# Decoder step on one core: VectorE subtracts the normalized stream, two bias tables behind one block each, six weight slots behind the skewed table's store

## The chip, the cores and the metric

The kernel runs on one core of a Trainium2 chip. The metric is the device time of one execution in microseconds (us), and lower is better. The kernel before took 2029.69 us (median of 3 runs, 2027.88 to 2030.03).

## What is computed

A two-layer decoder step over 576 tokens (one prompt of 512, eight sequences of 8 new tokens). Layer 0 mixes with a Mamba-2 state space scan, layer 1 with sparse attention; each is followed by a layer norm, an MLP with squared ReLU and another layer norm. All is float32. The part that matters here, cut from the reference:

```python
def layer_norm(x, g, b):
    xf = x.astype(jnp.float32)
    mu = jnp.mean(xf, axis=-1, keepdims=True)
    var = jnp.mean(jnp.square(xf - mu), axis=-1, keepdims=True)
    return ((xf - mu) * lax.rsqrt(var + LN_EPS)).astype(x.dtype) * g + b

def sq_relu_mlp(x, w1, w2):
    return jnp.square(jax.nn.relu(x @ w1)) @ w2

def run_group(...):
    ...
    for i in range(DEPTH):
        ...
        h = layer_norm(DN_ALPHA * h + mix, ln_g[i, 0], ln_b[i, 0])
        h = layer_norm(DN_ALPHA * h + sq_relu_mlp(h, mlp_w1[i], mlp_w2[i]), ln_g[i, 1], ln_b[i, 1])
```

The attention of layer 1 adds a bias that depends on the distance between two positions: `rel_bias` (32 buckets, 16 heads), looked up by `rel_bucket(dist)`.

## The kernel before

**Layout.** The residual stream `xT` lies in SBUF as 8 chunks of 128 features by 576 tokens. Every large projection goes over weight *slots* of 128x1024 floats (512 KB), streamed from HBM in one fixed order. One slot is the weights of 128 outputs over 1024 inputs.

**Precision.** A product is made of three: each operand is a rounded upper part plus the difference to it (the lower part), and `dense_block` (L1339) adds upper x upper, upper x lower and lower x upper, so one slot costs 48 matmuls of 288 columns. The upper part of a slot is made by ScalarE (`split_hi`, L975), the lower part, raw minus upper, by GpSimd (`split_lo`, L724). Slots lie in a ring of two: SyncE loads slot s+2 when slot s has been split (`stream`, L627), ScalarE rounds slot s when TensorE has used slot s-2, GpSimd subtracts, TensorE multiplies.

**One MLP** (`mlp`, `raw_projection` and `projection` on TensorE) goes in two halves of the 4096 hidden features: first product of half 0 (16 slots, one per block), second product of half 0 (8 blocks of 2 slots), first product of half 1, second product of half 1. The first product of half 0 starts on the stream before it is normalized; the layer norm's factors are put in behind the product. Meanwhile VectorE (`normalize`, L2172 and L2174) subtracts the mean and multiplies by the scale, chunk by chunk.

**The stretch in question** is the start of the second product of half 0, in layer 0 (slots called S+0 to S+15 here, S = `S_M2[k][0]`) and again in layer 1. Slots S+0 and S+1 are split inside the loop before. Then ScalarE (`mlp_his`, L1189 to L1209) makes for each of the 8 chunks two passes of `normalized`: one writes the rounded upper part of the normalized stream into `XM[k]` (L1184; `XM[0]` is `xs`, `XM[1]` is `xs_b`), one writes the float32 stream in place (L1185). It does five chunks, rounds slot S+2, does three chunks, rounds slot S+3. GpSimd (`mlp_los` with `x_los`, L837) makes the lower part of five chunks, then of slot S+2, then of three chunks, then of slot S+3. These lower parts are needed only by the first product of half 1, 14 slots later.

VectorE adds each finished block onto the stream (`residual`, L1969), in place; block 0 may be added when its chunk's lower part is made.

**Bias tables**, layer 0 only. Behind the second block, TensorE makes the strip table (three products into `bS` and `bXM`, L1672), VectorE copies it out (L2233 to L2235), TensorE then makes the compressed table into `bS` (L1677), VectorE copies it (L2237). SyncE stores the strip table (65 KB, L641), loads two slots, writes it 128 times over as a skewed table of 3 MB from HBM to HBM (L645), loads two slots, waits for that store, loads 2 MB of it as strips (L649), then stores and reloads the compressed table in small pieces (L656, L663) and copies 16 rows (L671), with two slots between each four of them. All this is in SyncE's one queue with the weights. The waits are semaphores written out by hand; nothing is scheduled by a planner.

Of the kernel before, what the change touches and what calls it, by code (L numbers as in the profile page):

```python
# [24 lines left out]
F32 = mybir.dt.float32  # L25
F32R = mybir.dt.float32r
I32 = mybir.dt.int32
ALU = mybir.AluOpType
# [5 lines left out]
KC = D // P  # L34
# [35 lines left out]
NSLOT = 2  # L70
# [15 lines left out]
def build(nc, a):  # L86

    with ExitStack() as ctx:
# [54 lines left out]
        xT = carve(KC, T)  # L143
# [473 lines left out]
        @block.sync  # L617
        def _(sp):
            for j in range(NSLOT):
                sp.dma_start(ring[:, j, :], a["w"][j, :, :]).then_inc(w_ready[j], 16)  # L620

            def stream(first, last):
                with sp.Fori(first // NSLOT, last // NSLOT) as i:
                    for j in range(NSLOT):

                        sp.wait_ge(w_split, i * NSLOT + (j + 1 - NSLOT))
                        sp.dma_start(ring[:, j, :], a["w"][i * NSLOT + j, :, :]).then_inc(w_ready[j], 16)  # L627

            for dst, name in PARAM_TILES[1:]:
                sp.dma_start(dst, a[name]).then_inc(s_par, 16)  # L630
            stream(NSLOT, S_OUT[0] + 2 * NSLOT)

            sp.wait_ge(xbc_ready, NXB)
            sp.wait_ge(y_gated, (MG - 1) * NT)
            sp.dma_start(xT, a["x"]).then_inc(x_back, 16)
            s_bias = S_M2[0][0] + 4 * NSLOT
            stream(S_OUT[0] + 2 * NSLOT, s_bias)


            sp.wait_ge(bt_ready, 1)  # L640
            sp.dma_start(a["bscr"], bt).then_inc(bt_stored, 16)  # L641
            stream(s_bias, s_bias + NSLOT)
            y0 = Y0 - 2 * P + 1
            sp.wait_ge(bt_stored, 16)
            sp.dma_start(a["bskew"], bass.AP(a["bscr"].tensor, y0, [[0, P], [XN, NH], [1, RW]])  # L645
                         ).then_inc(skew_stored, 16)
            stream(s_bias + NSLOT, s_bias + 2 * NSLOT)
            sp.wait_ge(skew_stored, 16)
            sp.dma_start(Rs, bass.AP(a["bskew"].tensor, P - 1, [[NH * RW - 1, P], [RW, NH], [1, RB]])  # L649
                         ).then_inc(strips_loaded, 16)  # L650


            s_next = s_bias + 2 * NSLOT
            sp.wait_ge(bt_ready, 2)
            for qa in range(8):
                sp.dma_start(bass.AP(a["bscr"].tensor, (7 - qa) * CS * NH, [[NH, CS], [8 * CS * NH, 8], [1, NH]]),  # L656
                             btT[qa * CS:(qa + 1) * CS]).then_inc(bt_stored, 16)
                if qa % 4 == 3:
                    stream(s_next, s_next + NSLOT)
                    s_next += NSLOT  # L660
            sp.wait_ge(bt_stored, 16 * 9)
            for pa in range(8):
                sp.dma_start(cbt[pa * CS:(pa + 1) * CS], bass.AP(a["bscr"].tensor, (63 - 55 - pa) * CS * NH,  # L663
                                                                 [[NH, CS], [CS * NH, NSIG], [1, NH]])
                             ).then_inc(cbt_ready, 16)
                if pa % 4 == 3:
                    stream(s_next, s_next + NSLOT)
                    s_next += NSLOT
            sp.wait_ge(strips_loaded, 16)
            for h in range(NH):  # L670
                sp.dma_start(nr[h * NS:(h + 1) * NS, :], Rs[0:NS, h, 0:P + 2 * NS]).then_inc(rows_loaded, 16)  # L671
                if h % 4 == 3:
                    stream(s_next, s_next + NSLOT)
                    s_next += NSLOT
            stream(s_next, S_O + 2 * NSLOT)

            sp.wait_ge(s_ptab, 16)

            for b in range(NB):
                buffer_free(sp, b, True)  # L680
                for pg in range(NPG):
                    page = sp.value_load(ptab[0:1, b * NPG + pg:b * NPG + pg + 1], min_val=0, max_val=NPHYS - 1)
                    sp.dma_start(skv[b % KVB][:, pg, :], a["sel"][page, :, :]).then_inc(kv_loaded[b % KVB], 16)
            stream(S_O + 2 * NSLOT, N_SLOTS)

            for m in range(0, KC, 2):
                sp.wait_ge(x_ready, 3 * KC + m + 2)
                sp.dma_start(a["o_y"][:, m:m + 2, :], xT[:, m:m + 2, :]).then_inc(x_out, 16)
            sp.wait_ge(x_out, 16 * KC // 2)
# [3 lines left out]
        def _(pool):  # L693
# [135 lines left out]
            pool.wait_ge(sd_stored, 16 * MG)  # L829
            pool.wait_ge(outs, 48)  # L830

            def x_los(k, first, last):


                for m in range(first, last):
                    pool.wait_ge(x_ready, 2 * k * KC + m + 1)
                    pool.tensor_tensor(XM[k][:, 1, m, :], xT[:, m, :], XM[k][:, 0, m, :].bitcast(F32), ALU.subtract  # L837
                                       ).then_inc(x_split, 1)

            def mlp_los(k, half, end):  # L840

                with pool.Fori(0, H1 // NSLOT) as i:
                    for j in range(NSLOT):
                        split_lo(S_M1[k][half] + 2 + j, i)

                        pool.wait_ge(hid_hi, i * NSLOT + ((2 * k + half) * H1 + j + 1))
                        m = i * NSLOT + j
                        pool.tensor_tensor(HID[k][1][:, m, :], sq[:, j, :], HID[k][0][:, m, :].bitcast(F32),
                                           ALU.subtract).then_inc(hid_ready, 1)
                if half:  # L850
                    finish_los(2 * k + 1)
                else:
                    s0 = S_M2[k][half] + 2
                    x_los(k, 0, 5)
                    split_lo(s0)
                    x_los(k, 5, KC)
                    split_lo(s0 + 1)
                    split_los(s0 + 2, end)


            pool.wait_ge(blk_evac, B_OUT[1] + KC)
# [100 lines left out]
        def _(act):  # L962
# [224 lines left out]
            def mlp_his(k, half, end):  # L1187
# [10 lines left out]
                if half:  # L1198
                    finish_his(2 * k + 1)
                else:  # L1200
                    s0 = S_M2[k][0] + 2
                    act.wait_ge(w_used, S_M2[k][0])
                    for m in range(5):
                        normalized(2 * k, m, XM[k])
                    split_hi(s0)
                    for m in range(5, KC):
                        normalized(2 * k, m, XM[k])
                    split_hi(s0 + 1)
                    split_his(s0 + 2, end)  # L1209

            root_of_variance(0)
# [128 lines left out]
        def _(pe):  # L1340
# [27 lines left out]
            def projection(b0, s0, blocks, nsl, hi, lo, ready=None, raw=0, between=None):  # L1368

                for j in range(2):  # L1370
                    dense_block(b0 + j, s0 + j * nsl, nsl, hi, lo, ready=ready if j == 0 else None, raw=raw)
                if between:
                    between()
                with pe.Fori(1, blocks // 2) as i:
                    for j in range(2):
                        dense_block(b0 + j, s0 + j * nsl, nsl, hi, lo, i, 2 * nsl, raw=raw)
# [285 lines left out]
                    mm = pe.matmul(flat_s[:, cols], ones[0:TQ, :], CEN[k][0:TQ, cols], start=True, stop=True)  # L1662
                mm.then_inc(ln_wide, 1)

            def bias_tables():

                pe.wait_ge(s_tab, 16 * N_ATT)
                pe.wait_ge(ln_scaled, 2 * KC)
# [1 line left out]
                for i, (bank, lo) in enumerate(((bS[:, 0, :], 0), (bS[:, 1, :], 512), (bX[:, :], 1024))):  # L1670
                    n = min(512, XN - lo)
                    pe.matmul(bank[0:NH, 0:n], relb[:, :], eb[:, lo:lo + n], start=True, stop=True  # L1672
                              ).then_inc(bt_done, 1)

                pe.wait_ge(bt_ready, 1)
                for i in range(8):
# [4 lines left out]
            def mlp(k):  # L1681

                raw_projection(2 * k, B_M1[k][0], S_M1[k][0], H1)
                projection(B_M2[k][0], S_M2[k][0], KC, 2, *HID[k], (hid_ready, 2 * k * H1),
                           between=bias_tables if k == 0 else None)
                pe.wait_ge(x_split, NORM_LO[k] + KC)
                projection(B_M1[k][1], S_M1[k][1], H1, 1, XM[k][:, 0], XM[k][:, 1])
                last_projection(2 * k + 1, *HID[k], (hid_ready, (2 * k + 1) * H1))
# [233 lines left out]
        def _(dve):  # L1922
# [179 lines left out]

            def residuals(k, between=None):

                b0, s0 = B_M2[k][0], S_M2[k][0]
                for j in range(2):
                    dve.wait_ge(x_split, NORM_LO[k] + j + 1)
                    residual(b0 + j, j, ALPHA, s0 + (j + 1) * 2)
                if between:
                    between()  # L2110
                with dve.Fori(1, KC // 2) as i:
                    for j in range(2):
                        dve.wait_ge(x_split, at_step(NORM_LO[k] + j + 1, i, 2))
# [113 lines left out]
                    if half == 0:  # L2227
                        normalize(2 * k, 0, i)

            def bias_tables():  # L2230

                dve.wait_ge(bt_done, 3)
                dve.tensor_copy(bt[:, 0:512], bS[0:NH, 0, :])  # L2233
                dve.tensor_copy(bt[:, 512:1024], bS[0:NH, 1, :])
                dve.tensor_copy(bt[:, 1024:XN], bX[0:NH, 0:XN - 1024]).then_inc(bt_ready, 1)  # L2235
                dve.wait_ge(cbt_done, 1)
                dve.tensor_copy(btT.rearrange("p s h -> p (s h)"), bS[:, 0, 0:8 * NH]).then_inc(bt_ready, 1)  # L2237

# [1 line left out]
            layer_norm(0)  # L2240
            mlp_hidden(0, 0)

            residuals(0, bias_tables)
            mlp_hidden(0, 1)
            last_residuals(1)
            layer_norm(1)
# [410 lines left out]
```

## Time and profile before

| | before |
|---|---|
| median of 3 runs | 2029.69 us (2027.88 to 2030.03) |
| the profiled execution | 2017.36 us, span 2015.7 us |
| TensorE busy | 1897.1 us, 94% of the span |
| VectorE, ScalarE, GpSimd busy | 983.7, 738.9, 889.7 us |
| mean granted TensorE clock | 0.97 |
| DMA | 185.14 MB, 92 GB/s mean |

The span is from the first to the last instruction of the profiled execution, and that execution's own time is 1.7 us more. [...] "Released by" is the instruction whose semaphore ended a wait. Matmul ends are modelled.

### The profile page before, as it was taken

The numbers are of one execution on the slowest core, as the hardware profiler recorded it, in microseconds if no ns is written. First come the engines' busy times: TensorE is split into PE (matmuls) and PEld (weight loads), VectorE is DVE, ScalarE is ACT, GpSimd is POOL, SyncE is SP. The second block draws the span as 40 slices with busy tenths as digits, with TensorE's granted clock in tenths as the row PEclk, the third lists the DMA queues.
The fourth block names the chain that finished last, engine by engine and source line by source line (L and its number), as shares of the span: only waits on it lengthen the run. The fifth ranks groups of instructions, "written<-read, shape, count | busy, mean of one in ns | idle before, by whom it ended". The sixth has DMA issues, their size and how long they took to land. (4 is left out here: it accounts for less than half of the span.)

```text
span 2015.7 us, 36867 instructions
## 1 busy us (share of the span) xinstructions
PE 1897.1 (94%) x14678; PEld 1738.9 (86%) x14678; DVE 983.7 (49%) x1762; ACT 738.9 (37%) x1346; POOL 889.7 (44%) x644
## 2 busy tenths in 40 slices
PE   8999989979899998999999999799879999999996
PEld 7987878758799988999999989555459999999996
DVE  6375866756576500121456731577457652012134
ACT  5474636532233431222221141466444334122222
POOL 3544343342475552565443323444305456346552
PEclk9999989989999999999999989799999999999998
DMA  5213113141322217522222434600431222222221
GB/s 188 66 64 112 68 42 126 53 152 53 111 86 83 75 64 181 131 75 83 84 74 83 145 104 106 230 1 1 143 132 63 73 83 74 76 82 83 84 79 62
DMA packets 61223, 185.14 MB, mean 92 GB/s; under 512 B 15662, under 2 KB 20430, under 8 KB 59568
## 3 DMA queue, kind: packets, MB, share of 16 engines
q1 hardware_dynamic: 50432, 130.92, 20.3%
q0 software_dynamic: 9952, 50.08, 7.2%
q10 hardware_dynamic: 720, 2.49, 0.3%
q8 instruction: 83, 1.36, 0.3%
q14 instruction: 36, 0.29, 0.0%
HBM read 167.05 MB, written 27.35 MB: 96 GB/s over the span
## 5 line engine op out<-in xcount | busy, mean ns | idle before, releaser
L1361 PE MATMUL dense<-xs,split 128*128 128x288 f32 x5056 | 722.7, 300 | 2.3 <-DVE xs L2461 2.3
L1361 PEld LDWEIGHTS dense<-xs,split 128*128 128x128 f32 x5056 | 693.7, 191 | 30.0 <-issue 29.9
L724 POOL TENSOR_TENSOR split<-ring,split 128x1024 fp32r<-128x1024 f32 x174 | 434.7, 2499 | 568.0 <-ACT split L975 567.9
L975 ACT ACTIVATE split<-ring 128x1024 fp32r<-128x1024 f32 x212 | 224.2, 1058 | 700.8 <-PE dense L1361 668.2
L1969 DVE SCALAR_TENSOR_TENSOR tile<-tile,dense 128x576 f32<-128x576 f32 (+1 forms) x56 | 42.2, 754 | 398.2 <-PE dense L1361 392.8
L1361 PE MATMUL dense<-hid,split 128*128 128x288 f32 x1536 | 214.9, 303 | 8.9 <-POOL split L724 8.9
L1361 PEld LDWEIGHTS dense<-hid,split 128*128 128x128 f32 x1536 | 213.6, 195 | 9.4 <-POOL split L724 5.8
L1361 PE MATMUL dense<-xs_b,split 128*128 128x288 f32 (+1 forms) x1440 | 193.8, 297 | 0.0
L1361 PEld LDWEIGHTS dense<-xs_b,split 128*128 128x128 f32 x1440 | 193.6, 189 | 0.0
L1361 PE MATMUL dense<-hid_b_hi,split 128*128 128x288 f32 x1024 | 181.5, 298 | 3.4 <-POOL split L724 3.4
L1361 PEld LDWEIGHTS dense<-hid_b_hi,split 128*128 128x128 f32 x1024 | 152.8, 191 | 3.6 <-issue 3.6
L949 POOL TENSOR_SCALAR tile<-tile,tile,tile 128x128 f32<-128x128 f32 (+3 forms) x128 | 78.3, 626 | 81.0 <-DVE tile L2395 81.0
L764 POOL TENSOR_TENSOR tile<-tile,tile 128x512 f32<-128x512 f32 (+1 forms) x20 | 25.9, 1294 | 197.3 <-DVE tile L2031 197.2
L1361 PE MATMUL dense<-hid_b_lo,split 128*128 128x288 f32 x512 | 111.1, 298 | 0.0
L2210 DVE TENSOR_SCALAR sq<-dense 128x576 f32<-128x576 f32 x32 | 24.3, 758 | 155.9 <-PE dense L1361 155.9
L1957 DVE SCALAR_TENSOR_TENSOR tile<-tile,tile,tile 128x512 f32<-128x512 f32 x72 | 78.6, 1092 | 25.5 <-ACT tile L1070 23.8
L714 POOL TENSOR_TENSOR segment_terms<-triu,a_split 128x1024 fp32r<-128x1024 f32 (+1 forms) x40 | 85.3, 2152 | 0.0
L2216 DVE TENSOR_TENSOR sq<-sq 128x576 f32<-128x576 f32 x64 | 71.4, 1116 | 28.1 <-ACT sq L1194 27.0
L1361 PEld LDWEIGHTS dense<-hid_b_lo,split 128*128 128x128 f32 x512 | 84.4, 192 | 0.0
L1265 ACT ACTIVATE tile<-tile,tile 128x128 f32<-128x128 f32 (+3 forms) x128 | 70.5, 553 | 17.8 <-DVE tile L2380 17.6
L1737 PE MATMUL dense<-tile,tile 128*128 128x128 f32 x576 | 66.4, 274 | 0.9 <-issue 0.8
L1737 PEld LDWEIGHTS dense<-tile,tile 128*128 128x128 f32 x576 | 64.9, 188 | 1.9 <-issue 1.1
(355 smaller groups left out, 2662.1 us busy)
## 6 DMA issues: line engine op xcount, KB each, us to landing
ring<-in_w SPq DMA_DIRECT2D x212, 512.0 KB, 3.3
tile<-in_state POOLq DMA_DIRECT2D x4, 2048.0 KB, 8.8
o_sssm<-tile POOLq DMA_DIRECT2D x4, 2048.0 KB, 8.6
tile<-in_cmp POOLq DMA_DIRECT2D x32, 256.0 KB, 3.2
tile<-in_win POOLq DMA_DIRECT2D x8, 1024.0 KB, 5.9
tile<-in_sel SPq DMA_DIRECT2D x32, 256.0 KB, 5.3
o_kv<-tile POOLq DMA_DIRECT2D x1, 3456.0 KB, 12.0
bskew<-bscr SPq DMA_DIRECT2D x1, 3072.0 KB, 22.6
```

What stands on the lines that cost most here:

```text
L714: last = pool.tensor_tensor(AT[0:L, part, :, 0:L], triu[0:L, c // 4, 0:L].unsqueeze(1).to_broadcast([L, HPG, L]), over_heads(a_hl[0:L, par ...
L724: pool.tensor_tensor(split[:, j, 1, :], ring[:, j, :], split[:, j, 0, :].bitcast(F32), ALU.subtract).then_inc(w_split, 1)
L764: pool.tensor_tensor(heads(xdec[0:L, :], MP), heads(xdt[0:L, :], MP), over_heads(dec_tok[0:L, c, g * HPG:(g + 1) * HPG], L, MP), ALU.mult) ...
L949: last = pool.tensor_scalar(pb(u, r)[:, 0:n], pb(u, r)[:, 0:n], wt[:, u % 2, r:r + 1], gate, ALU.mult, ALU.mult)
L975: act.activation(split[:, j, 0, :], ring[:, j, :], ACT.Copy).then_inc(w_hi, 1)
L1265: last = act.activation(pb(u, r)[:, 0:n], pb(u, r)[:, 0:n], ACT.Exp, bias=nmx[:, u % 4, r:r + 1], accum_out=sm[:, u % 4, r:r + 1])
L1361: mm = pe.matmul(dense[:, 2 * par + h_, 0:n], split[:, j, w, cols], v[:, kk, h_ * HT:h_ * HT + n], start=kk == 0 and t == 0, stop=kk == ns ...
L1737: mm = pe.matmul(dense[:, 2 * (s_ % 2) + kv, r * P:(r + 1) * P], cw1[:, kv, r, j, :], rows, start=j == 0, stop=j == 7)
L1957: dve.scalar_tensor_tensor(o[:, 0:NP_TOK], r[:, k:k + NP_TOK], cw[:, x, k:k + 1], o[:, 0:NP_TOK], ALU.mult, ALU.add)
L1969: dve.scalar_tensor_tensor(xm, xm, alpha, dense_out(blk % 2), ALU.mult, ALU.add).then_inc(blk_evac, 1)
L2210: dve.tensor_scalar(halves(h), dense_out(j), 0.0, None, ALU.max).then_inc(blk_evac, 1)
L2216: dve.tensor_tensor(h, h, h, ALU.mult).then_inc(hid_sq, 1)
```

## The change

1. In both layers the eight subtractions for the lower parts of the normalized stream go from GpSimd (`x_los`, gone) to VectorE, at the head of `residuals`. GpSimd now splits slots S+2 and S+3 in the plain loop.
2. ScalarE rounds slot S+2 behind two chunks (five before) and slot S+3 behind six (eight before).
3. The strip table is made behind the first block of the second product, the compressed table behind the second block, on TensorE and on VectorE. Both stood behind the second block.
4. SyncE loads six slots (two before) between the store of the skewed table and the wait for it.

```diff
-            stream(s_bias + NSLOT, s_bias + 2 * NSLOT)
+            stream(s_bias + NSLOT, s_bias + 4 * NSLOT)
             sp.wait_ge(skew_stored, 16)
             sp.dma_start(Rs, ...).then_inc(strips_loaded, 16)
-            s_next = s_bias + 2 * NSLOT
+            s_next = s_bias + 4 * NSLOT
...
                 else:
                     s0 = S_M2[k][half] + 2
-                    x_los(k, 0, 5)
-                    split_lo(s0)
-                    x_los(k, 5, KC)
-                    split_lo(s0 + 1)
-                    split_los(s0 + 2, end)
+                    split_los(s0, end)
...
                     act.wait_ge(w_used, S_M2[k][0])
-                    for m in range(5):
+                    for m in range(KC):
+                        if m in (2, 6):
+                            split_hi(s0 + m // 4)
                         normalized(2 * k, m, XM[k])
-                    split_hi(s0)
-                    for m in range(5, KC):
-                        normalized(2 * k, m, XM[k])
-                    split_hi(s0 + 1)
                     split_his(s0 + 2, end)
...
                 for j in range(2):
                     dense_block(b0 + j, s0 + j * nsl, nsl, hi, lo, ...)
-                if between:
-                    between()
+                    if between:
+                        between[j]()
...
             def residuals(k, between=None):
+                for m in range(KC):
+                    dve.wait_ge(x_ready, 2 * k * KC + m + 1)
+                    dve.tensor_tensor(XM[k][:, 1, m, :], xT[:, m, :], XM[k][:, 0, m, :].bitcast(F32), ALU.subtract
+                                      ).then_inc(x_split, 1)
                 for j in range(2):
                     dve.wait_ge(x_split, NORM_LO[k] + j + 1)
                     residual(b0 + j, j, ALPHA, s0 + (j + 1) * 2)
-                if between:
-                    between()
+                    if between:
+                        between[j]()
```

How the instructions stand on ScalarE at the start of the second product of layer 0 (`tile_49` is the stream, `split<-ring` the upper part of a weight slot). Before, from the fourth chunk on:

```order
L1184 ACTIVATE xs<-tile_49,lnb,lng 128x576
L1185 ACTIVATE tile_49<-tile_49,lnb,lng 128x576
L1184 ACTIVATE xs<-tile_49,lnb,lng 128x576
L1185 ACTIVATE tile_49<-tile_49,lnb,lng 128x576
L975 ACTIVATE split<-ring 128x1024
L1184 ACTIVATE xs<-tile_49,lnb,lng 128x576
```

Now, from the second chunk on:

```order
L1172 ACTIVATE xs<-tile_49,lnb,lng 128x576
L1173 ACTIVATE tile_49<-tile_49,lnb,lng 128x576
L963 ACTIVATE split<-ring 128x1024
L1172 ACTIVATE xs<-tile_49,lnb,lng 128x576
L1173 ACTIVATE tile_49<-tile_49,lnb,lng 128x576
```

The rounding of slot S+2 stands three chunks earlier, and that of slot S+3 two.

VectorE at the same place (`tile_126` is the strip table, `tile_118` the compressed one). Before:

```order
L2174 TENSOR_TENSOR tile_49<-tile_49,bS 128x576
L2224 REGISTER_ALU
L2224 COMPARE_AND_BRANCH
L1969 SCALAR_TENSOR_TENSOR tile_49<-tile_49,dense 128x576 x2
L2233 COPY tile_126<-bS 16x512
L2234 COPY tile_126<-bS 16x512
L2235 COPY tile_126<-bXM 16x16
L2237 COPY tile_118<-bS 128x128
```

Now:

```order
L2167 TENSOR_TENSOR tile_49<-tile_49,bS 128x576
L2217 REGISTER_ALU
L2217 COMPARE_AND_BRANCH
L2096 TENSOR_TENSOR xs<-tile_49,xs 128x576 x8
L1957 SCALAR_TENSOR_TENSOR tile_49<-tile_49,dense 128x576
L2226 COPY tile_126<-bS 16x512
L2227 COPY tile_126<-bS 16x512
L2228 COPY tile_126<-bXM 16x16
L1957 SCALAR_TENSOR_TENSOR tile_49<-tile_49,dense 128x576
L2232 COPY tile_118<-bS 128x128
```

The eight subtractions stand ahead of block 0's addition, and the strip table's copies between the two additions.

TensorE, blocks 0 and 1 (96 matmuls each). Before:

```order
L1361 MATMUL dense<-hid,split 128x288 x192
L1672 MATMUL bS<-tile_125,tile_129 16x512 x2
L1672 MATMUL bXM<-tile_125,tile_129 16x16
L1677 MATMUL bS<-tile_129,tile_124 128x16 x8
L1374 UNCONDITIONAL_BRANCH
```

Now:

```order
L1347 MATMUL dense<-hid,split 128x288 x96
L1658 MATMUL bS<-tile_125,tile_129 16x512 x2
L1658 MATMUL bXM<-tile_125,tile_129 16x16
L1347 MATMUL dense<-hid,split 128x288 x96
L1665 MATMUL bS<-tile_129,tile_124 128x16 x8
L1360 UNCONDITIONAL_BRANCH
```

Block 1 now lies between the strip table's products and the compressed table's, which need VectorE's copy of the first.

## Rows read from the trace of the kernel before

**Rows 1.** Who waited for whom on TensorE (total us, times, longest)

```profile
PE dense L1361 <- POOL split L724: 12.3, 3, 5.6
```

**Rows 2.** Timeline, layer 0: start us, us, engine, line, operation, [idle before <- releaser]

```profile
700.28 13.17 PE L1361 MATMUL dense<-hid,split 128*128 128x288 f32 x96
705.36 0.86 ACT L1184 ACTIVATE xs<-tile,lnb,lng 128x576 fp32r<-128x576 f32 x1
...
712.95 1.04 ACT L975 ACTIVATE split<-ring 128x1024 fp32r<-128x1024 f32 x1
...
714.29 2.35 POOL L724 TENSOR_TENSOR split<-ring,split 128x1024 fp32r<-128x1024 f32 x1
...
716.78 14.66 PE L1361 MATMUL dense<-hid,split 128*128 128x288 f32 x96 [3.34 <-POOL split L724]
...
724.99 1.06 ACT L975 ACTIVATE split<-ring 128x1024 fp32r<-128x1024 f32 x1 [5.50 <-PE dense L1361]
```

**Rows 3.** Timeline, the bias tables behind block 1

```profile
731.38 1.89 PE L1672 MATMUL bS<-tile,tile 128*16 128x512 f32 x4
...
734.76 1.96 PE L1677 MATMUL bS<-tile,tile 128*128 128x16 f32 x16 [1.45 <-DVE tile L2235]
...
736.57 40.76 PE L1361 MATMUL dense<-hid,split 128*128 128x288 f32 x288
...
744.86 1.06 ACT L975 ACTIVATE split<-ring 128x1024 fp32r<-128x1024 f32 x1 [12.31 <-PE dense L1361]
```

**Rows 4.** Timeline, the same place in layer 1

```profile
1680.52 0.85 ACT L1184 ACTIVATE xs_b<-tile,lnb,lng 128x576 fp32r<-128x576 f32 x1
...
1689.44 2.34 POOL L724 TENSOR_TENSOR split<-ring,split 128x1024 fp32r<-128x1024 f32 x1
...
1691.93 0.50 PE L1361 MATMUL dense<-hid_b_hi,split 128*128 128x288 f32 x2 [3.43 <-POOL split L724]
...
1700.16 1.06 ACT L975 ACTIVATE split<-ring 128x1024 fp32r<-128x1024 f32 x1 [5.51 <-PE dense L1361]
```

**Rows 5.** Stretches: from:to, length, busy of PE, PEld, DVE, ACT, POOL, clock, DMA, GB/s

```profile
717.00:721.00 4.00, 4.00 (x21) 4.00 (x22) 0.00 (x0) 2.49 (x4) 4.00 (x4) 0.62 0.41 131
736.60:740.00 3.40, 3.40 (x18) 3.40 (x18) 0.29 (x1) 0.00 (x0) 0.00 (x0) 0.58 0.39 153
1565.00:1585.00 20.00, 19.61 (x151) 18.41 (x151) 11.06 (x16) 4.44 (x6) 6.08 (x3) 1.00 0.25 80
```

**Rows 6.** One line's instructions: duration ns min/median/max, first and last start

```profile
L1928 DVE TENSOR_TENSOR xs<-tile,xs x8: 750/755/760, 8.6 to 15.6; 128x576 fp32r<-128x576 f32 x8
```

**Rows 7.** Timeline of a layer norm, VectorE and GpSimd together

```profile
1541.95 2.40 POOL L724 TENSOR_TENSOR split<-ring,split 128x1024 fp32r<-128x1024 f32 x1 [2.35 <-ACT split L975]
...
1542.44 2.53 DVE L2136 TENSOR_TENSOR row<-row,tile 128x576 f32<-128x576 f32 x1
...
1548.37 0.76 DVE L2136 TENSOR_TENSOR row<-row,tile 128x576 f32<-128x576 f32 x1
...
1548.39 3.00 POOL L724 TENSOR_TENSOR split<-ring,split 128x1024 fp32r<-128x1024 f32 x1 [2.13 <-ACT split L975]
```

**Rows 8.** SyncE's queue: issue of the skewed table's store and of the next weights

```profile
755.46 0.63 SPq L645 DMA_DIRECT2D bskew<-bscr  x1
...
761.41 6.84 SPq L627 DMA_DIRECT2D ring<-in_w  x2
```

**Rows 9.** DMA issues by line: KB, us from issue to landing

```profile
bskew<-bscr SPq DMA_DIRECT2D x1, 3072.0 KB, 22.6
tile<-bskew SPq DMA_DIRECT2D x1, 2048.0 KB, 8.9
```

**Rows 10.** Timeline, the end of the skewed table's store

```profile
779.38 1.06 ACT L975 ACTIVATE split<-ring 128x1024 fp32r<-128x1024 f32 x1 [13.95 <-DMA ring<-in_w]
...
782.91 9.80 PE L1361 MATMUL dense<-hid,split 128*128 128x288 f32 x53 [5.58 <-POOL split L724]
...
792.06 1.06 ACT L975 ACTIVATE split<-ring 128x1024 fp32r<-128x1024 f32 x1 [10.36 <-PE dense L1361]
```

More of the change, by code:

```diff
@@ L830, in _ @@
             pool.wait_ge(outs, 48)
[L832 to L838, printed above, removed]
             def mlp_los(k, half, end):
@@ L1663, in spread_scale, with strip_tables @@
                 mm.then_inc(ln_wide, 1)
-            def bias_tables():
+            def strip_tables():
                 pe.wait_ge(s_tab, 16 * N_ATT)
@@ L1673, in bias_tables, with compressed_tables @@
                               ).then_inc(bt_done, 1)
+            def compressed_tables():
                 pe.wait_ge(bt_ready, 1)
@@ L1684, in mlp @@
                 projection(B_M2[k][0], S_M2[k][0], KC, 2, *HID[k], (hid_ready, 2 * k * H1),
-                           between=bias_tables if k == 0 else None)
+                           between=(strip_tables, compressed_tables) if k == 0 else None)
                 pe.wait_ge(x_split, NORM_LO[k] + KC)
@@ L2228, in mlp_hidden, with strip_tables @@
                         normalize(2 * k, 0, i)
-            def bias_tables():
+            def strip_tables():
                 dve.wait_ge(bt_done, 3)
@@ L2235, in bias_tables, with compressed_tables @@
                 dve.tensor_copy(bt[:, 1024:XN], bX[0:NH, 0:XN - 1024]).then_inc(bt_ready, 1)
+            def compressed_tables():
                 dve.wait_ge(cbt_done, 1)
@@ L2241, in _ @@
             mlp_hidden(0, 0)
-            residuals(0, bias_tables)
+            residuals(0, (strip_tables, compressed_tables))
             mlp_hidden(0, 1)
```

## The prediction

> **What bounds the kernel now.** TensorE is busy for 94% of the span, so only what stops it or slows it counts. The first view is therefore who TensorE waited for. Its largest entry is the dense projections waiting for GpSimd's lower parts of weight slots: 12.3 us in three waits, the longest of 5.6 [rows 1]. The timeline places them: 3.34 us in front of slot S+2 in layer 0 [rows 2], 3.43 us at the same place in layer 1 [rows 4], and 5.58 us behind the skewed table's store [rows 10]. A fourth stop of 1.45 us stands between the two bias tables, where TensorE waits for VectorE's copy [rows 3].
>
> A stop costs more than its own length, which one sees from the distance between a restart and the moment ScalarE is released by the end of the slot. A slot at full clock takes 6.49 us: behind the tables TensorE runs six slots in 40.76 us, the first ends at 744.86, and the other five share the remaining 32.47 [rows 3]. The first slot after a stop takes 8.21 us in layer 0 (716.78 to 724.99) [rows 2], 8.23 in layer 1 [rows 4] and 8.29 behind the tables [rows 3]. [...] So each stop takes 1.72, 1.74 and 1.80 us more.
>
> **The waits in front of slot S+2 (parts 1 and 2).** In layer 0 ScalarE begins the stream's chunks at 705.36 and rounds S+2 at 712.95, so one chunk takes 1.52 us and a rounding 1.04 [rows 2]. GpSimd subtracts from 714.29 to 716.64; block 0 had ended at 713.45 [rows 2]. Now the rounding stands behind two chunks: it starts at 705.36 + 3.04 = 708.4 and ends at 709.45, and GpSimd, with nothing else to do, is finished at about 711.9. That is 1.5 us ahead of need. In layer 1 everything starts at 1680.52 [rows 4]: rounding 1683.56 to 1684.6, GpSimd done at 1687.0, needed at 1691.93 - 3.43 = 1688.5. The margin is again 1.5. Both waits go: **3.34 + 1.72 + 3.43 + 1.74 = 10.23 us**.
>
> What is late next is slot S+3. ScalarE reaches it after six chunks and one rounding, 10.16 us after its start: in layer 1 at 1690.7, rounded at 1691.7, subtracted at 1694.15 with 2.35 to 2.40 us for GpSimd. TensorE asks at 1688.5 + 6.49 = 1695.0. The margin is 0.9 us; in layer 0, where the strip table's matmuls come in between, it is 2.9. I charge nothing.
>
> **The subtractions on VectorE.** The form exists at the start of the kernel: 755 ns each [rows 6], eight are 6.0 us, cheaper than on GpSimd. They come at ScalarE's pace of one in 1.52 us. The last chunk is ready at 705.36 + 8 x 1.52 + 2 x 1.04 = 719.6 in layer 0, so block 0's addition, at once before, runs at about 720.5, and the table copies behind it end at about 722.3. The next who needs either is TensorE behind block 1, at 713.45 + 1.89 + 2 x 6.49 = 728.3. So 6 us cover this; in layer 1 the cover is much the same. Cost: nothing on the path.
>
> VectorE and GpSimd hinder each other here. An addition of 0.76 us took 2.53 when it started inside a GpSimd subtraction, and a GpSimd subtraction that started 0.02 us after such an addition took 3.00 in place of 2.40 [rows 7]. So whoever starts second waits, and GpSimd's split can lose about one VectorE operation, 0.66 us. That leaves 0.2 of the 0.9 us margin in layer 1. The lower bound of this cost is 0; the upper bound, with two operations ahead of it (1.5), is a wait of 0.6. I take 0, since by the times above the sixth subtraction ends at 1691.5, before GpSimd starts at 1691.8.
>
> [...]
>
> **The tables (part 3).** The products stay: 1.89 and 1.96 us [rows 3]. With block 1 in between, VectorE's copy is 6 us early and the wait of 1.45 goes. The clock is the unsure part. Before, 1.89 us of strip products, 1.45 of idleness and 1.96 of sixteen-column products came in a row, and then it was low (0.58) [rows 5]. In layer 1's layer norm short products for token sums interrupt the dense ones several times within 20 us, and the clock stays at 1.00 [rows 5]. The halves of the tables, apart, are nearest to that. I take the whole 1.80 back; the other end is rival A. Gain: **1.45 + 1.80 = 3.25 us**.
>
> **The skewed table (part 4).** The 3 MB take 22.6 us [rows 9]. SyncE issues the next weights 5.95 us after them [rows 8], because the ring's slot is free only then, and they are there just after the table: at 779.38, 23.9 us after its issue [rows 10]. The wait for the table in SyncE's queue holds nothing up, since the third load has to wait for GpSimd's split of that first late slot anyway. Everything here hangs on TensorE's pace and moves forward with it, the early strip table included, because two slots' loads are issued between its store and the skewing. So the stall of 5.58 us and its clock loss of 792.06 - 782.91 - 6.49 = 2.66 [rows 10] remain: gain 0.
>
> The load of the strips moves four slots later, to the issue of S+15. It lands 8.9 us after issue [rows 9], the next weights are issued 6.5 behind it, and a weight load has 12.4 us until TensorE feels it (779.38 - 761.41 = 17.97, less the 5.58 that it cost [rows 8, 10]). The small pieces of the compressed table follow four slots later too, each group behind its own two loads. Cost 0; the upper bound is rival E.
>
> **Sum.** 10.23 + 3.25 = 13.5 us off the profiled execution's 2017.36 gives 2003.9. The median of the runs was 2029.69, 12.3 above the profiled execution, and no view says where those lie; I take the same difference off it: **2016.2 us**. Below 0.2%, 4 us, a measurement of this kernel can't be told from no change.
>
> **Rivals.**
>
> A. The low clock stays. The short products, not the idleness, lower it, and they now come at two places: 1.80 is not given back and about 1.75 is paid once more. For it: 16 columns per matmul and 0.58 behind them. Against it: the 1.00 in the layer norm [rows 5]. Gain 9.9, time 2019.8. [...]
>
> B. Slower: GpSimd starves. VectorE's stream of subtractions wins again and again, and slot S+2's lower part comes behind the eighth. In layer 1 that is 1694.8 + 0.75 + 2.35 = 1697.9, a wait of 9.4 in place of 3.43; in layer 0 it is 722.7 against a need at 715.3, 7.4 in place of 3.34. With the tables' 3.25 the net is 10.0 - 3.25 = 6.8 us slower, 2036.5. It decides from the point at which GpSimd starts S+2 in layer 1 later than 1686.15. Against it: a subtraction every 1.52 us leaves half the time free, and GpSimd's worst seen is 3.00 us [rows 7].
>
> C. The change does not do what it should: the wait only moves to slot S+3 at about its old length, with the clock loss. The margin of 0.9 is for it, the arithmetic against. Only the tables' 3.25 is gained: 2026.4, no measurable difference.
>
> D. The six loads do relieve the stall behind the skewed table: 5.58 + 2.66 more, 2008.0. For it: it is the change's own fourth part. Against it: those loads wait for the ring.
>
> E. The strips' load or the small pieces meet the 2 MB of compression weights that GpSimd's queue fetches behind slot S+17, and a stall like the skewed table's appears in the first product of half 1: 8.2 back, 2024.4.
>
> **How the numbers follow.** Forecast 0.65, A 0.14, B 0.04, C 0.07, D 0.04, E 0.06. The forecast's own range is 2013 to 2018.5: the skew's clock loss may come out at 1.7 in place of 2.66, the layer 1 margin may cost 0.6, and the three runs before lay 2.15 apart. The range of 2012.0 to 2024.5 takes in A and E and leaves out B, C and D, 0.15 together. Faster by over 0.2%: forecast, A, D and two thirds of E, 0.87. Within: C and the rest of E, 0.09. Slower: B, 0.04.
>
> **What the profile would show.** Right: TensorE waits for GpSimd once, for about 5.6 us, behind the skewed table; no wait before slot S+2 or S+3; the compressed table's products without a wait; slots of 6.5 us at all three places. Wrong: a wait for GpSimd in front of S+3 (C) or S+2 (B) with the split longer than 3 us; a first slot of over 8 us behind either table (A); no wait behind the skewed table (D); a new wait 100 us later (E).

## The result, and the profile after

The changed kernel took 2011.48 us (median of 5 runs, 2005.92 to 2015.54) against 2027.88 for the kernel before (5 runs beside it, 2022.51 to 2030.03). The ratio is 0.9924, 95% interval [0.9899, 0.9949]. That is clear of the 0.2% that was named as the bound. The forecast of 13.5 us off 2029.69 is a ratio of 0.9933, inside that interval. As a time, 2011.48 lies 4.7 us below the 2016.2 that was forecast and 0.5 us below the range's lower end of 2012.0: the kernel before ran 1.8 us faster beside it than in the three runs that were shown, and the other 2.9 us are gain beyond the 13.5.

The two profiled executions alone would tell another story, with spans of 2015.7 and 2013.4 us. So the first thing to read is the place itself. Who TensorE waited for, after:

```profile
PE dense L1347 <- POOL split L724: 6.2, 1, 6.2
```

Three waits of 12.3 us [rows 1] have become one. The timeline of layer 0 after, where rows 2 and 3 stood:

```profile
701.52 13.17 PE L1347 MATMUL dense<-hid,split 128*128 128x288 f32 x96
...
706.59 0.85 ACT L1172 ACTIVATE xs<-tile,lnb,lng 128x576 fp32r<-128x576 f32 x1
...
709.63 1.04 ACT L963 ACTIVATE split<-ring 128x1024 fp32r<-128x1024 f32 x1
...
710.75 2.40 POOL L724 TENSOR_TENSOR split<-ring,split 128x1024 fp32r<-128x1024 f32 x1 [2.65 <-ACT split L963]
...
714.62 1.89 PE L1658 MATMUL bS<-tile,tile 128*16 128x512 f32 x4
...
716.49 13.28 PE L1347 MATMUL dense<-hid,split 128*128 128x288 f32 x96
...
717.78 2.40 POOL L724 TENSOR_TENSOR split<-ring,split 128x1024 fp32r<-128x1024 f32 x1 [4.62 <-ACT split L963]
...
721.45 0.75 DVE L1957 SCALAR_TENSOR_TENSOR tile<-tile,dense 128x576 f32<-128x576 f32 x1
...
723.31 0.15 DVE L2228 COPY tile<-bXM 16x16 f32<-16x16 f32 x1
...
729.61 1.86 PE L1665 MATMUL bS<-tile,tile 128*128 128x16 f32 x16
...
731.31 39.27 PE L1347 MATMUL dense<-hid,split 128*128 128x288 f32 x288
...
738.11 1.06 ACT L963 ACTIVATE split<-ring 128x1024 fp32r<-128x1024 f32 x1 [7.24 <-PE dense L1347]
```

No bracket with GpSimd stands on a TensorE row. GpSimd's lower part of S+2 is done at 713.15, 1.5 us before TensorE leaves block 0 for the strip products and 3.3 us before the matmuls that need it (716.49). That of S+3 is done at 720.18, and TensorE asks for it about 6.5 us after 716.49. VectorE's last copy of the strip table ends at 723.46, TensorE asks at 729.6. From the start of the second product to the release of ScalarE at the end of the fifth slot, 44.58 us (700.28 to 744.86 [rows 2, 3]) have become 36.59 (701.52 to 738.11).

GpSimd and ScalarE in layer 1 after, where rows 4 stood:

```profile
1681.95 0.86 ACT L1172 ACTIVATE xs_b<-tile,lnb,lng 128x576 fp32r<-128x576 f32 x1
...
1686.11 2.40 POOL L724 TENSOR_TENSOR split<-ring,split 128x1024 fp32r<-128x1024 f32 x1 [2.66 <-ACT split L963]
...
1693.14 2.40 POOL L724 TENSOR_TENSOR split<-ring,split 128x1024 fp32r<-128x1024 f32 x1 [4.63 <-ACT split L963]
...
1696.43 1.06 ACT L963 ACTIVATE split<-ring 128x1024 fp32r<-128x1024 f32 x1 [0.33 <-PE dense L1347]
```

The split of S+2 ends at 1688.51, before block 1 begins at about 1689.9. The split of S+3 ends at 1695.54, and ScalarE's release at 1696.43 marks the end of slot S+2: the margin of 0.9 us is there as worked out. VectorE's new rows:

```profile
L2096 DVE TENSOR_TENSOR xs<-tile,xs x8: 759/760/1551, 708.2 to 720.8; 128x576 fp32r<-128x576 f32 x8
L2096 DVE TENSOR_TENSOR xs_b<-tile,xs_b x8: 757/759/1551, 1683.6 to 1696.1; 128x576 fp32r<-128x576 f32 x8
```

0.76 us at the median and 1.55 at most: the two subtractions of each layer that start inside a split (at 712.22 and 719.25, 1687.59 and 1694.6) take 1.55 us and end 0.6 us behind it. GpSimd's four splits here started first, and they keep 2.40 us.

The skewed table, after (TensorE's wait, and the DMA issues; rows 8 to 10 before):

```profile
776.75 41.94 PE L1347 MATMUL dense<-hid,split 128*128 128x288 f32 x288 [6.17 <-POOL split L724]
```

```profile
bskew<-bscr SPq DMA_DIRECT2D x1, 3072.0 KB, 23.1
tile<-bskew SPq DMA_DIRECT2D x1, 2048.0 KB, 9.0
```

It stalls as before, 6.17 us in place of 5.58.

**Where the profiled executions' gain went.** The first product of half 1 starts 5.9 us earlier than before (818.52 against 824.38), and at the end of the span 2.3 us are left, although layer 1 gained its 5 us. The loss is in places where the change moves no work of the compute engines. From the start of the first product of half 1 in layer 0 to the start of the second product of half 0 in layer 1 it took 851.1 us before (824.38 to 1675.43) and 858.3 after (818.52 to 1676.86). Three stretches of before, then of after (columns as in rows 5):

```profile
1505.00:1512.00 7.00, 3.64 (x128) 2.87 (x126) 1.21 (x2) 3.08 (x8) 0.00 (x0) 1.00 0.01 2
1512.00:1530.00 18.00, 17.61 (x118) 17.16 (x119) 7.92 (x11) 7.63 (x12) 4.39 (x2) 0.91 0.10 30
1565.00:1590.00 25.00, 24.61 (x188) 23.41 (x188) 15.14 (x20) 6.83 (x9) 9.55 (x5) 1.00 0.20 64
```

```profile
1505.00:1512.00 7.00, 4.35 (x83) 3.62 (x75) 1.76 (x3) 3.30 (x7) 0.00 (x0) 0.50 0.01 2
1512.00:1530.00 18.00, 18.00 (x116) 17.52 (x116) 6.76 (x9) 6.39 (x9) 4.48 (x2) 0.87 0.09 30
1565.00:1590.00 25.00, 24.65 (x177) 23.17 (x176) 13.61 (x20) 6.83 (x9) 7.99 (x5) 0.93 0.20 64
```

The columns to read are the clock (third from the end, a share of full speed) and the busy TensorE: between attention and the output projection this execution was granted 0.50 where the other had 1.00, and again less behind 1565 (0.93 against 1.00). The same 32 matmuls (L1909, L1897) take 1.15 us from 1508.93 before and 1.98 us from 1506.87 after, so 2.1 us of the lead are left there; the products for token sums (L1662, L1648) start at 1581.86 before and 1583.29 after, 1.4 us late. These stretches hold 3.5 us of the loss; 3.8 us lie earlier and 1.4 us behind layer 1's second product, and these were not placed. In second executions of the same two kernels (below) the 851.1 and 858.3 us were 854.4 and 855.0, so a difference of this size comes and goes without an edit.

### The profile page after: what moved, and what is told of

Same layout as the page of the kernel before. It is cut to its first block and busy times, and to the rows that moved or that the text cites. A ratio compares the mean times of both kernels' runs of the same rounds, so it can differ in the third digit from the quotient of the medians.

```text
span 2013.4 us, 36880 instructions
## 1 busy us (share of the span) xinstructions
PE 1900.6 (94%) x14678; PEld 1742.1 (87%) x14678; DVE 997.4 (50%) x1778; ACT 738.4 (37%) x1346; POOL 867.9 (43%) x628
```

## The experiments

Each was timed in five rounds beside the kernel before, if nothing else is said; the ratios are to that kernel.

**Parts 1 and 2 alone** (the edit is the change's first two parts on the kernel before).

> Parts 1 and 2 alone (VectorE subtracts the stream's lower parts, ScalarE rounds slots S+2 and S+3 earlier), tables and SyncE's queue as before. Theory (the waits in front of S+2 go, with the clock loss behind them): no wait for GpSimd at S+2 in either layer; 5.1 us less in layer 0's and 5.2 in layer 1's second product; the tables' stop of 1.45 and the stall behind the skewed table (5.6) as before; about 10 us below the kernel before. Rival (the median's gain of 16 us comes mostly from the tables or the queue): 5 us or less.

Measured: 2012.96 us, ratio 0.9946 [0.9927, 0.9965], some 11 us. TensorE's waits, the table's and the skewed table's are left:

```profile
PE dense L1347 <- POOL split L724: 6.1, 1, 6.1
```

```profile
700.06 26.17 PE L1347 MATMUL dense<-hid,split 128*128 128x288 f32 x192
...
729.54 1.96 PE L1663 MATMUL bS<-tile,tile 128*128 128x16 f32 x16 [1.45 <-DVE tile L2225]
731.35 39.26 PE L1347 MATMUL dense<-hid,split 128*128 128x288 f32 x288
```

Blocks 0 and 1 run as one piece of 26.17 us. The wait of 1.45 is still there, yet the six slots behind the tables take 39.26 us in place of 40.76: the clock didn't fall behind this stop (1.00 was granted in the first 3 us behind the tables, 0.59 in the kernel before). That was not expected, and the last two experiments take it up.

**Part 3 alone.**

> Part 3 alone (strip table behind block 0, compressed table behind block 1). Theory: the strip products (1.9 us) fill a part of the 3.34 wait at S+2, which shrinks to about 1.4 to 1.5; in addition VectorE's copy is done early, so the 1.45 wait goes; the low clock behind the tables goes with it (first slot 6.8 or less in place of 8.3). About 5 us less in layer 0, layer 1 as before with its 3.4 wait. Rival (short products lower the clock): first slot behind either table 8 us or more, gain 3 or less.

Measured: 2018.09 us, ratio 0.9972 [0.9958, 0.9985], some 6 us.

```profile
713.35 1.89 PE L1672 MATMUL bS<-tile,tile 128*16 128x512 f32 x4
...
716.76 13.25 PE L1361 MATMUL dense<-hid,split 128*128 128x288 f32 x96 [1.48 <-POOL split L724]
729.86 1.86 PE L1679 MATMUL bS<-tile,tile 128*128 128x16 f32 x16
731.56 39.27 PE L1361 MATMUL dense<-hid,split 128*128 128x288 f32 x288
```

As expected, the strip products fill 1.9 of the 3.34 us. The rest of 1.48 costs only itself: the two slots behind it take 13.25 us, where a stop of 3.34 had made them 14.66 [rows 2]. The compressed table's products follow without a wait. The stretch from the second product's start to the fifth slot's end is 38.10 us (700.25 to 738.35), 6.5 less than before; parts 1 and 2 alone give 38.08, all together 36.59. So the parts overlap in layer 0 and don't add up there. Layer 1 keeps a wait of 3.45.

**Part 4 alone.**

```diff
-            stream(s_bias + NSLOT, s_bias + 2 * NSLOT)
+            stream(s_bias + NSLOT, s_bias + 4 * NSLOT)
...
-            s_next = s_bias + 2 * NSLOT
+            s_next = s_bias + 4 * NSLOT
```

> Part 4 alone (six slots between the skewed table's store and the wait for it). Theory: nothing, within 0.2% of the kernel before; the stall behind the skewed table stays at 5.6 to 6.2 us, since the next weights' bytes follow the 3 MB in the same queue and the third load waits for the ring. Rival (the wait in SyncE's queue held the weights up): the stall falls below 2 us, 8 us faster.

Measured: 2028.68 us, ratio 1.0017 [1.0004, 1.0030]. The stall is 5.91 us, so the rival is out. The small loss was tested from the other side:

**The changed kernel without part 4.**

> The changed kernel with part 4 undone (two slots behind the skewed table's store, as before). Theory (part 4 gives nothing and costs nothing): within 0.2% of the changed kernel. Rival (the 0.17% that part 4 cost alone is its own): about 3 us faster than the changed kernel.

Measured: 2010.15 us, ratio 0.9930 [0.9916, 0.9944], beside 0.9918 [0.9905, 0.9931] for the changed kernel timed beside it. Taking part 4 away brings nothing, so its cost of 0.17% alone is not confirmed; the part is worth nothing that these runs can tell.

**GpSimd keeps the subtractions, in the new order** (VectorE's loop of eight is gone).

```diff
                     s0 = S_M2[k][half] + 2
-                    split_los(s0, end)
+                    x_los(k, 0, 2)
+                    split_lo(s0)
+                    x_los(k, 2, 6)
+                    split_lo(s0 + 1)
+                    x_los(k, 6, KC)
+                    split_los(s0 + 2, end)
```

> The changed kernel, but GpSimd keeps the eight subtractions, in the new order (two chunks, slot S+2, four chunks, slot S+3, two chunks). Theory (the order of the splits was what mattered, not the engine): S+2 is in time in both layers; S+3 is done about 2 us ahead in layer 0 and within 0.5 us of need in layer 1; time within 0.2% of the changed kernel. Rival (VectorE is needed): a wait of 1 us or more for GpSimd at S+3 in layer 1, with the clock loss behind it 3 us or more slower than the changed kernel.

Measured: 2010.39 us, ratio 0.9926 [0.9906, 0.9945], the changed kernel's own (0.9924). The only wait for GpSimd that the view of waits lists in the dense projections is the skewed table's, 5.2 us. The timeline shows one more, at slot S+3 in layer 1:

```profile
1694.52 1.08 PE L1360 MATMUL dense<-hid_b_hi,split 128*128 128x288 f32 x4
...
1695.07 0.30 PEld L1360 LDWEIGHTS dense<-hid_b_hi,split 128*128 128x128 f32 x2 [0.35 <-POOL split L724]
```

Four matmuls that take 0.70 us elsewhere take 1.08, and the weight load among them (PEld) waits 0.35 us for GpSimd's split, which ends at 1695.01. So the margin of 0.9 us has turned into a wait of about 0.4, without a slow slot behind it. That is all that the runs show VectorE's subtractions to give; the rest of the gain doesn't need them.

**ScalarE's old order, VectorE subtracts.**

```diff
-                    for m in range(KC):
-                        if m in (2, 6):
-                            split_hi(s0 + m // 4)
+                    for m in range(5):
                         normalized(2 * k, m, XM[k])
+                    split_hi(s0)
+                    for m in range(5, KC):
+                        normalized(2 * k, m, XM[k])
+                    split_hi(s0 + 1)
```

> The changed kernel with ScalarE's old order (slot S+2 rounded behind five chunks, S+3 behind eight); VectorE still subtracts. Theory (ScalarE's order is what brought S+2 in time): a wait of about 3.2 us at S+2 in layer 1 and of about 1.2 us in layer 0, where the strip products fill the rest; the clock loss of 1.7 us in layer 1; 5 us slower than the changed kernel. Rival (GpSimd's subtractions were what made S+2 late): no wait above 0.5 us, same time as the changed kernel.

Measured: 2017.03 us, ratio 0.9962 [0.9950, 0.9974], 9 us slower than the changed kernel beside it. The waits are back:

```profile
718.33 13.24 PE L1349 MATMUL dense<-hid,split 128*128 128x288 f32 x96 [1.26 <-POOL split L724]
```

```profile
1690.10 0.51 PE L1349 MATMUL dense<-hid_b_hi,split 128*128 128x288 f32 x2 [3.24 <-POOL split L724]
```

1.26 and 3.24 us, close to the 1.2 and 3.2 expected. With the clock loss in layer 1 that makes 6.2 of the 9 us; by the two intervals the 9 us are uncertain by some 3.6, and the rest is not accounted for. So the gain needs ScalarE's new order.

Whether ScalarE's order alone would do was not tested: each run that has it also took GpSimd's split of S+2 out from behind the five subtractions. Before, that split waited for them:

```profile
711.61 2.73 POOL L837 TENSOR_TENSOR xs<-tile,xs 128x576 fp32r<-128x576 f32 x2 [0.31 <-ACT tile L1185]
714.29 2.35 POOL L724 TENSOR_TENSOR split<-ring,split 128x1024 fp32r<-128x1024 f32 x1
```

ScalarE had rounded the slot by 713.99. With the rounding moved ahead of three chunks, the fifth chunk would reach GpSimd 1.04 us later, so with GpSimd's order as before an estimate from these rows puts the split's start at about 715.3 and the wait at 4.4 us in place of 3.34. By this estimate the change lives on two things: the roundings' place in ScalarE's order, which the run shows, and no later chunks ahead of the splits on GpSimd, which no run tests alone. Which engine subtracts hardly matters.

**The changed kernel again.**

> The changed kernel once more, for the others of this call. Theory: 0.992 to 0.994 of the kernel before; the stretch from the start of the second product to the fifth slot's end in layer 0 within 0.1 us of the first profile (36.6 us), while the span differs by several us through low-clock stretches in places that the change does not touch. Rival (the rest of the span is as steady as that stretch): span within 1 us of 2013.4.

Measured: 2008.04 us, ratio 0.9918 [0.9905, 0.9931]. The stretch of layer 0 is 36.59 us again (703.69 to 740.28), while the second product starts 2.2 us later than in the first profile and the span is 2009.0 in place of 2013.4. So the stretch is steady to 0.1 us and the rest is not.

**The skewed table in four pieces.**

```diff
-            sp.dma_start(a["bskew"], bass.AP(a["bscr"].tensor, y0, [[0, P], [XN, NH], [1, RW]])
-                         ).then_inc(skew_stored, 16)
-            stream(s_bias + NSLOT, s_bias + 4 * NSLOT)
-            sp.wait_ge(skew_stored, 16)
+            for q in range(4):
+                sp.dma_start(a["bskew"][:, 4 * q:4 * q + 4, :],
+                             bass.AP(a["bscr"].tensor, y0 + 4 * q * XN, [[0, P], [XN, 4], [1, RW]])
+                             ).then_inc(skew_stored, 16)
+                stream(s_bias + (q + 1) * NSLOT, s_bias + (q + 2) * NSLOT)
+            sp.wait_ge(skew_stored, 64)
...
-            s_next = s_bias + 4 * NSLOT
+            s_next = s_bias + 5 * NSLOT
```

The load of the strips thereby moves two slots further back.

> The changed kernel with the skewed table stored in four pieces of four heads (768 KB each), two weight slots loaded behind each piece. Theory (the stall is the weights' place behind 3 MB in the queue): a piece takes about 5.7 us, so the next weights land in time; no wait for GpSimd anywhere in layer 0's second product, the slot behind takes 6.5 us; 8 us faster than the changed kernel. Rival (the table's traffic as a whole slows the weights, wherever it stands): four waits of 1 to 2 us each, gain 2 us or less.

Measured: 2002.17 us, ratio 0.9897 [0.9882, 0.9913], some 6 us ahead of the changed kernel beside it. TensorE and the DMA issues:

```profile
730.93 78.27 PE L1349 MATMUL dense<-hid,split 128*128 128x288 f32 x576
809.04 31.13 PE L1349 MATMUL dense<-xs,split 128*128 128x288 f32 x231
```

```profile
ring<-in_w SPq DMA_DIRECT2D x15, 512.0 KB, 3.3
bskew<-bscr SPq DMA_DIRECT2D x4, 768.0 KB, 6.8
```

Twelve slots run without a gap, from 730.93 to 809.04, 78.1 us; the same twelve took 731.31 to 818.52, 87.2 us, in the changed kernel. The difference of 9.1 us is the stall of 6.17 and the slow slot behind it (2.97 us over 6.49). A piece took 6.8 us, not the 5.7 expected. In the medians 6 of the 8 us expected arrive, which the two intervals allow. The same 3 MB go over the same queue, so it was the weights' place behind them that cost: those issued 6.1 us into the uncut table landed 18.3 us after their issue (the changed kernel), those between the pieces 3.3 at the median.

**In two halves.** The same edit with two pieces of eight heads, so four slots lie between the first piece and the load of the strips.

> The changed kernel with the skewed table in two halves of 1.5 MB, two weight slots behind each. Theory (a weight load may land up to 12.4 us after its issue without TensorE feeling it): a half takes 11 to 12 us, the weights issued 6 us into it land about 7 us after their issue, so there is no stall, as with four pieces; same time as the pieces. Rival (the pieces won because each was shorter than the distance of two loads): a wait of 1 us or more, with the clock loss 3 us slower than the pieces.

Measured: 2004.08 us, ratio 0.9894 [0.9873, 0.9914], the pieces' value. A half lands after 13.2 us (11 to 12 were expected), and there is no wait. The weights issued 5.9 us into each half landed 8.4 us after their issue (7 were expected), within the 12.4 that were worked out from before. Behind the uncut table they took 17.9 us (before) and 18.3 (after).

**Pieces, and GpSimd keeps the subtractions.** Both edits above.

> The skewed table in four pieces, and GpSimd keeps the stream's subtractions in the new order. Theory: no wait for GpSimd in the dense projections of either layer, like the pieces with VectorE's subtractions; within 0.2% of it, about 0.990 of the kernel before. Rival (VectorE's subtractions give something that only shows without the stall): 2 us or more slower than the pieces.

Measured: 2000.51 us, ratio 0.9882 [0.9862, 0.9903]. It is the fastest kernel of the study, though its interval overlaps that of the pieces.

**The clock behind the tables, once more** (one execution each, not timed in rounds).

> Parts 1 and 2 alone, a second look at the clock behind the tables. Theory (the fall behind the tables needs the stop at S+2 15 us earlier; without it the 1.45 stop and the short products leave the clock high): first slot behind the tables 6.8 us again. Rival (whether it falls is chance, from run to run): 8.3 us in this or in another look.

> The kernel before, a second look. Theory (as above): first slot behind the tables 8.3 us again. Rival (chance): 6.8 us. In either case the two waits at S+2 are 3.3 and 3.4 us, and that behind the skewed table 5 to 6.5.

The theory fell in both. Parts 1 and 2 alone, second execution:

```profile
730.86 2.15 PE L1663 MATMUL bS<-tile,tile 128*128 128x16 f32 x16 [1.45 <-DVE tile L2225]
732.84 40.64 PE L1347 MATMUL dense<-hid,split 128*128 128x288 f32 x288
```

The kernel before, second execution:

```profile
739.79 1.96 PE L1677 MATMUL bS<-tile,tile 128*128 128x16 f32 x16 [1.45 <-DVE tile L2235]
741.60 39.26 PE L1361 MATMUL dense<-hid,split 128*128 128x288 f32 x288
```

The first kernel has the low clock this time (40.64; 0.50 was granted in the first 3 us) and the second hasn't (39.26; 1.00), each the other way round than in its first profile. With part 4 alone it was 40.76 (0.59). So in five profiles with the 1.45 us stop the clock fell in three. There the first of the six slots takes 8.1 to 8.3 us; in the other two it takes 6.78 and 6.79. In the nine with the tables apart it took 6.79 or 6.80 us in every one. A fall thus costs 1.5 us (40.76 against 39.26).

## Why the prediction was right

**The waits in front of S+2: right.** Both went. In layer 0 the split of S+2 ended 1.5 us before the end of block 0, as worked out; since the strip products come next, the real margin was 3.3 us. In layer 1 it ended 1.4 us before block 1. The margin at S+3 in layer 1 was 0.9 us. The 10.23 us stand against some 11 for parts 1 and 2 alone (interval 7 to 15).

**The subtractions on VectorE: right, but beside the point.** They cost nothing, as worked out. What the prediction did not say, and the runs show, is that they gain next to nothing either: with GpSimd subtracting in the new order the time is the same but for a wait of 0.4 us, and with VectorE subtracting under ScalarE's old order two of the waits return. The prediction named the three parts of the edit together as the cause of the gain.

**The tables: the mechanism right, the clock term mis-sized.** The wait of 1.45 went. The 1.80 us "back" was wrong in two ways. It measured the slow slot (8.29) against 6.49, the pace inside a run of slots; but the first slot behind the short products takes 6.79 even when the clock stays high, so 1.50 can come back. And it was read from one execution. The loss behind this stop is there in three of five executions, so what the change gives back is about 0.9 us on average (three fifths of 1.50), and 1.50 or nothing in one pair. The prediction called it the unsure part and had looked for the doubt in the short products (rival A). They are not it: in nine profiles with short products alone the clock stayed high (1.00 in the first 3 us behind the compressed table). The doubt was in the executions.

**The skewed table: right.** The stall stayed, 6.17 us, and lay between 5.0 and 6.5 in the eleven profiles that store the table in one piece; the slot behind it lost 1.8 to 3.0 us over 6.49. Part 4 gives nothing.

**Sum.** With 0.9 in place of 1.80 the forecast would have been 12.6 us. Measured were 15.4 us (the ratio 0.9924 of 2027.88), with an interval of 10 to 20, and 16.6 us with an interval of 14 to 19 when it was timed again (0.9918). The profiles place 13.3 us. From the start of the second product of half 0 to the start of the next product, layer 0 took 121.9 to 124.3 us in the three profiles with the old order throughout and 115.0 to 117.0 in four with the new one; layer 1 took 108.4 to 109.6 and 103.3 to 103.7. The means differ by 7.9 and 5.4. The mechanism accounts for that much. The 2 to 3 us beyond it are in no stretch that was read, and their cause stays open.

**The rivals.** A (low clock from short products), B (GpSimd starves), C (the wait moves to S+3) and D (the six loads relieve the stall) are each contradicted by rows above. B needed the split of S+2 in layer 1 to start 5.6 us or more after ScalarE's first chunk (1686.15 - 1680.52); it started 4.2 us after it (1686.11 - 1681.95) and took 2.40 us. VectorE's 0.76 us became 1.55 when it came second, and GpSimd kept its 2.40. E (a new stall from the strips' load meeting the compression weights) did not come: where the small reads of the compressed table met those 2 MB they landed in 9.2 to 9.8 us at the median (the five profiles with part 4 and an uncut table) in place of 5.1 to 5.3 (the kernels with the old queue). The 2 MB took 9.4 to 9.8 us in place of 8.5. The two do meet, then, but TensorE did not wait.

**The profiled pair.** The prediction took the profiled execution as a fair stand-in for the median. As a base for the sum it was fair. As a pair, 2015.7 and 2013.4 us would have shown a sixth of the gain; the second profile of before had a span of 2021.8, the second of the changed kernel 2009.0.

## What to carry to other kernels

When a weight stream is prepared by a chain of engines in program order, look first at where the chain's first link stands among the other work of its engine: here the gain came from moving two roundings on ScalarE, and with them the splits on GpSimd, ahead of work that is needed 14 slots later, whether VectorE or GpSimd did the subtractions. A large transfer in the same queue as a just-in-time stream was worth cutting into pieces with the stream's loads between them (two pieces did as well as four); a longer run of loads behind it did nothing, because the ring decides when they may go (the first one went 5.95 us after the table's issue in the kernel before and 6.09 after it in the changed kernel). Judge a change of under 1% by its own stretch in the trace and by several rounds, not by the spans of two executions.

## What the runs showed of the hardware

**The clock behind a short stop is not repeatable.** A stop of 1.45 us between short products was followed by a stretch at the lower level in three of five executions, at a cost of 1.5 us. Stops of 3.2 to 3.5 us were followed by it in all eight that were read: the slot behind them took 8.2 to 8.3 us in seven and 9.4 in one (layer 1, part 4 alone), in place of 6.5. Stops of 1.26 and 1.48 us behind the strip products were not followed by it (6.8 us for the next slot). The levels seen are 1.00 and 0.50 of full speed: of 4031 stretches of half a microsecond in the kernel before, 3771 were granted 1.00 and 226 were granted 0.50, with 34 in between. Behind the stop of 3.34 us it was 0.50 from 717 to 720 us, with 5 or 6 matmuls in each microsecond, and 1.00 from 721 on, with 9 or 10.

**A store from HBM to HBM of the same 3 MB** took 22.0 to 23.5 us in the eleven profiles, and the stall behind it differed by 1.5 us among them (by 0.5 to 0.9 us between two executions of one kernel). The weights issued 5.9 us behind it landed some 1.2 us after it. Cut in four, a piece of 768 KB landed in 6.8 us, and the weights between them in 3.3 us at the median, as elsewhere in the kernel. Cut in two, a piece landed in 13.2 us and the weights behind it in 8.4.
